# Kernel change: the last product's first weight unit is summed in DRAM and split early, with two output weightings in another order

## The chip, the cores and the metric

The kernel runs on one core of one Trainium2 chip. The metric is the device time of one execution in microseconds; the figure before is the median of three runs.

## The reference, cut to what matters

One layer: a token mixer with three gated branches, then a squared-ReLU MLP, each between RMS norms, over 512 tokens of 1024 channels in float32. The change lies in the MLP and the output.

```python
h = rms_norm(x, norm_ffn_pre[l])
f = jnp.square(jax.nn.relu(h @ w_ff1[l])) @ w_ff2[l]      # (512, 1024) @ (1024, 4096), then @ (4096, 1024)
x = x + rms_norm(f, norm_ffn_post[l])
```

## The kernel before, in words

**Numbers.** Each float32 operand is split in two parts: ScalarE copies it to a rounded "hi" part (`copy_hi`, L699), VectorE subtracts to get the "lo" part (`lo`, L1101), and TensorE makes three matmuls for each pair, hi by hi, hi by lo, lo by hi (L1621, L1623, L1625 in `products`; L1816, L1818, L1820 in `up_unit`).

**Weight units.** Weights come as units of 128 x 1024 values (512 KB). A unit is loaded from DRAM to one of ten slots in SBUF, split into one of four ring places of `w_hi` and `w_lo` (`RING = 4`), and used. The counts `w_hi_ready`, `w_lo_ready` and `unit_done` run over all units in order.

**The MLP.** The hidden width is worked in four quarters (`q`), each with a first matrix (`UP`, `w_ff1`) and a second one (`DOWN`, `w_ff2`). Each of these eight matrix products is made by a seven-product scheme of the Strassen kind over 2 x 2 blocks. `ORDER` gives the order: UP 1, 2, 5, 3, 6, 7, 4 and DOWN 5, 1, 2, 3, 6, 7, 4. A product needs a set of activations (a block, or a sum or difference of blocks, also split hi and lo, `set_hi`, `set_lo`) and a weight block or a sum of weight blocks in two units (h = 0, 1). The sums of weights come about in two ways: those of products 5 and 7 are made ahead in DRAM (`weight_sums`), during the mixer, by a plain copy issued on ScalarE's queue and a DMA with addition issued by GpSimd (`second_block`, L610); those of products 6 and 4 by adding one more block with such a DMA (`add_block`, L676) on top of the sum that already lies in the slot, once its split is done. The slots that DOWN 5, 6 and 4 use are 8 and 9 (`raw_d`), those of UP 5, 6 and 4 are 4 and 5 (in `glu`). So DOWN 4 of a quarter multiplies by the sum of all four blocks.

**Order of work.** Every engine's program is written out by hand. On ScalarE and VectorE, `split_behind(q, f, product, h)` splits the unit that comes four units later, once the unit named is done (for DOWN, once the product is done): behind UP 6 come the units of UP 4, behind UP 7 those of DOWN 5, behind UP 4 those of DOWN 1, behind DOWN 6 those of DOWN 4. SyncE's queue issues the loads in order (`ff_load`), each behind a wait for the split that frees its slot. A DOWN product is made in two tiles, t = 0 and 1, of 128 tokens by 512 columns each, 12 matmuls a tile; both need both units.

**The end.** In the last quarter each square (128 tokens `c` by half the columns) of the MLP's sum is finished by its last product: product 6 for c = 2 and 3, second half, product 7 for c = 0 and 1, second half, product 4 for c = 0 and 1, first half. Per tile VectorE adds the tile to the sum (`add_product`, L1463), ScalarE squares and sums it (`sum_squares`, L725) and, when a row block is whole, takes a root (L1093). VectorE multiplies each half by the norm's gain (`weigh`, L1468), takes the reciprocal of the root (L1477), scales, adds the residual and so releases the output DMA (`finish`, L1480, L561). `finish(n)` treats row block `FINAL[n]`, in the order 2, 3, 0, 1.

**Room.** `a_hi` and `a_lo` hold three differences of x blocks in the MLP; the second one, "21-22-11", is read by UP 6 alone.

Of the kernel before, what the change touches and what calls it, by code (L numbers as in the profile page):

```python
# [30 lines left out]
P = 128  # L31
# [63 lines left out]
MATRICES = 2 * QUARTERS  # L95
SLOTS = 10


# [131 lines left out]
def build(nc, x_d, xt_d, units_d, cols_d, rows_d, ws_d, bs_d, wsr_d, out_d):  # L230
    kept_d = nc.dram_tensor("mixed_kept", (SEQ, D), F32, kind="Internal").ap()
    made_d = nc.dram_tensor("weight_sums", (MATRICES * MADE_UNITS, P, D), F32, kind="Internal").ap()
    col_sums_d = nc.dram_tensor("spatial_sums", (KT, P), F32, kind="Internal").ap()
    with ExitStack() as ctx:
# [108 lines left out]
        last_weighted = {2: end[:, 1, :], 3: end[:, 2, :], 0: end[:, 3, :], 1: over("end_a", [P, D], "a_hi")}  # L343


        raw_loaded = [sem(f"raw_loaded{n}") for n in range(SLOTS)]
        first_copied = [sem(f"first_copied{f}") for f in range(2)]
        made = {product: sem(f"made{product}") for product in MADE}
        raw_added = [sem(f"raw_added{n}") for n in range(SLOTS)]
# [111 lines left out]
        def _(sp):  # L461
# [72 lines left out]
            for q in range(QUARTERS):  # L534
                if q == 1:
                    behind_sums(0, DOWN, 6)
                if q:
                    for product in (5, 1, 2, 3):
                        if product == 1:
                            ff_load(q, UP, 1, (0,))  # L540
                            behind_sums(q - 1, DOWN, 4)
                            ff_load(q, UP, 1, (1,))
                        else:
                            ff_load(q, UP, product)
                    ff_load(q, UP, 7)
                for product in (5, 1, 2, 3):
                    if q == 0 and product == 5:
                        behind_sums(0, UP, 6)
                    ff_load(q, DOWN, product)
                ff_load(q, DOWN, 7)  # L550
            sp.wait_ge(unit_done, ff_unit(QUARTERS - 1, UP, 4, 1) + 1)
# [14 lines left out]
        def _(pool):  # L566
# [37 lines left out]
            def second_block(m, product):  # L604
# [7 lines left out]
                               accum_op=ALU.add, max_dma_last_dim=SUM_BYTES).then_inc(made[product], 16)  # L612

            def mask_spatial(slot, loads):

                pool.wait_ge(spatial_loaded[slot], loads)
                nc.gpsimd.affine_select(out=ws_raw[:, slot, :], in_=ws_raw[:, slot, :],
                                        compare_op=ALU.is_ge, fill=0.0, base=0, pattern=[[1, P]],
                                        channel_multiplier=-1).then_inc(ws_masked, 1)
# [47 lines left out]
            for m in range(KT // 2, MATRICES):  # L667
                pool.wait_ge(unit_done, U_GATE + 2 * (KT + m) + 2)
                second_block(m, 7)

            def add_block(q, f, product, halves=(0, 1)):
# [11 lines left out]
            for q in range(QUARTERS):  # L683
                for f in range(2):
                    add_block(q, f, 6)
                    add_block(q, f, 4)

# [9 lines left out]
        def _(act):  # L697
# [11 lines left out]
            def ff_hi(u, into=None, free=True):  # L709
# [7 lines left out]
                if free:  # L717
                    act.wait_ge(unit_done, u + 1 - RING)
                copy_hi(w_hi[:, u % RING, :] if into is None else into, slots[slot]).then_inc(w_hi_ready, 1)

# [255 lines left out]
            def split_behind(q, f, product, h):  # L976
                u = ff_unit(q, f, product, h) + RING
                if u < UNITS:
                    ff_hi(u)
# [23 lines left out]
            for q in range(QUARTERS):  # L1003
# [46 lines left out]
                for h in range(2):  # L1050
                    done(q, UP, 7, h)
                    split_behind(q, UP, 7, h)
                act.wait_ge(hidden_diff, 4 * q + 1)
                set_hi(q, "22-21")
# [43 lines left out]
        def _(dve):  # L1098
# [12 lines left out]
            def ff_lo(u, into=None, hi=None):  # L1111

                dve.wait_ge(w_hi_ready, u + 1)
                lo(w_lo[:, u % RING, :] if into is None else into, slots[ff_slot(u)],
                   w_hi[:, u % RING, :] if hi is None else hi).then_inc(w_lo_ready, 1)

# [308 lines left out]
            def split_behind(q, f, product, h):  # L1425
                u = ff_unit(q, f, product, h) + RING
                if u < UNITS:
                    ff_lo(u)
# [57 lines left out]
            for q in range(QUARTERS):  # L1486
# [65 lines left out]
                split_behind(q, UP, 7, 1)  # L1552
                set_lo(q, "22-21")
                set_lo(q, "11")
                done(q, UP, 4, 0)
# [15 lines left out]
                for n, product in enumerate(ORDER[DOWN]):  # L1571
# [12 lines left out]
                    if q == QUARTERS - 1 and product == 4:  # L1584
                        dve.wait_ge(mlp_sum, sums_after(q, product, 0))
                        weigh(0, 0)
                        weigh(0, 1)
                        dve.wait_ge(out_weighted, 6)
# [17 lines left out]
                    elif product == 7:  # L1606
                        finish(1)
                    elif product == 4:
                        weigh(1, 1)
                        dve.wait_ge(mlp_sum, sums_after(q, product, 1))  # L1610
# [7 lines left out]
        def _(pe):  # L1618
# [207 lines left out]
            def down_tile(q, product, t):  # L1826
# [4 lines left out]
                for k in range(CH):  # L1831
                    u = ff_unit(q, DOWN, product, k // 2)
                    w = slice(k % 2 * HALF, (k % 2 + 1) * HALF)
                    mm = products(down_bank(q, product) + t, hi[:, k, at], low[:, k, at],
                                  w_hi[:, u % RING, w], w_lo[:, u % RING, w], k == 0 and not again,
                                  k == CH - 1, again)
# [24 lines left out]
            for q in range(QUARTERS):  # L1861
# [7 lines left out]
                for product in ORDER[DOWN]:  # L1869
                    for h in range(2):  # L1870
                        ready(Count(ff_unit(q, DOWN, product, h)))
                    pe.wait_ge(set_lo_ready, len(H_ORDER) * q + H_ORDER.index(SET_OF[product]) + 1)
# [63 lines left out]
```

## Time and profile before

| | |
|---|---|
| median of 3 runs | 953.14 us (953.08 to 953.18) |
| the profiled execution, its own time | 953.15 us |
| its span in the profile | 951.4 us (1.75 us of the time lie around it) |
| TensorE busy | 942.5 us, 99% |
| VectorE, ScalarE, GpSimd busy | 718.6, 431.8, 102.9 us |
| granted TensorE clock, mean | 0.999 of full speed (2.4 GHz) |

Times in the views are microseconds from the start of the span. In a timeline a line shows the start, the busy time, the engine, the source line, what is written and read and how many instructions are merged; in square brackets is the idle time before it and what ended that. The busy time of a VectorE or ScalarE instruction is a little longer than the distance to the next start when instructions follow each other without a pause, so distances between starts are used for chains.

### The profile page before, as it was taken

To read this page: it belongs to the slowest core of one execution; us is meant where nothing else is said; L and a number is where in the kernel's file an instruction comes from. 1 tells how busy PE (TensorE), PEld (TensorE's weight loads), DVE (VectorE), ACT (ScalarE), POOL (GpSimd) and SP (SyncE) were. 2 spreads that over 40 slices of the span, in tenths; PEclk is the share of its full clock that TensorE was granted. 3 is DMA by queue.
4 is the path that set the end of the run, shared out by engine and by line. 5 is a ranking of instruction groups with operands and counts; after the bars stand their busy time and mean duration, and the time that the engine had idled before them with its cause. 6 is when DMAs were issued, how large, how long until landed. Compare 5 with 4: busy or idle time off the path is not lost.

```text
span 951.4 us, 13451 instructions
## 1 busy us (share of the span) xinstructions
PE 942.5 (99%) x4824; PEld 807.5 (85%) x4824; DVE 718.6 (76%) x844; ACT 431.8 (45%) x536; POOL 102.9 (11%) x135
## 2 busy tenths in 40 slices
PE   9999999999999999999999999999999999999997
PEld 7888888888888888888888888899889989989985
DVE  5579879888888988886584444599975875786698
ACT  6543333333333322224374323377745745754774
POOL 1211001001100012222200000120001001100100
PEclk9999999999999999999999999999999999999999
DMA  8447558656755724454477323538586756848664
GB/s 319 141 160 229 172 169 229 186 189 193 196 187 176 199 89 132 132 134 153 134 194 248 111 89 112 198 129 236 167 253 133 235 171 154 229 133 244 187 191 132
DMA packets 41228, 168.01 MB, mean 177 GB/s; under 512 B 4953, under 2 KB 5089, under 8 KB 38881
## 3 DMA queue, kind: packets, MB, share of 16 engines
q1 hardware_dynamic: 31872, 111.85, 32.5%
q0 software_dynamic: 7680, 35.13, 20.8%
q10 hardware_dynamic: 1632, 20.45, 5.8%
q8 instruction: 27, 0.44, 0.2%
q14 instruction: 17, 0.13, 0.1%
HBM read 163.22 MB, written 37.75 MB: 211 GB/s over the span
## 4 chain that ended last, share of the span: by engine, by line
PE 97%; DVE 1%; DMA 1%; issue 0%; ACT 0%; SPq 0%; DVEq 0%
PE ps L1621 26%; PE ps L1625 26%; PE ps L1623 26%; PE ps L1816 6%; PE ps L1818 6%; PE ps L1820 6%; PE ps L1751 1%; DMA glu<-xt_in 1%; PE ps L1666 0%; DVE w_lo L1101 0%; DVE wide L1480 0%; DVE end L1468 0%; DVE wide L1463 0%; ACT c_hi L737 0%; DVE end_a L1468 0%
## 5 line engine op out<-in xcount | busy, mean ns | idle before, releaser
L1101 DVE TENSOR_TENSOR w_lo<-raw,w_hi 128x1024 fp32r<-128x1024 f32 (+1 forms) x141 | 172.3, 1227 | 93.8 <-ACT w_hi L699 93.5
L699 ACT ACTIVATE w_hi<-raw 128x1024 fp32r<-128x1024 f32 (+1 forms) x140 | 146.1, 1052 | 202.2 <-PE ps L1625 118.3
L1621 PE MATMUL ps<-a_hi,w_hi 128*128 128x512 f32 x576 | 224.9, 390 | 0.0
L1625 PE MATMUL ps<-a_hi,w_lo 128*128 128x512 f32 x576 | 224.2, 389 | 0.0
L1623 PE MATMUL ps<-a_lo,w_hi 128*128 128x512 f32 x576 | 224.1, 389 | 0.0
L1189 DVE SCALAR_TENSOR_TENSOR conf<-glu,cols,conf (+1 forms) x240 | 186.8, 778 | 27.5 <-DVE conf L1189 26.4
L1625 PEld LDWEIGHTS ps<-a_hi,w_lo 128*128 128x128 f32 x576 | 108.1, 188 | 22.6
L1623 PEld LDWEIGHTS ps<-a_lo,w_hi 128*128 128x128 f32 x576 | 108.2, 188 | 22.2
L1621 PEld LDWEIGHTS ps<-a_hi,w_hi 128*128 128x128 f32 x576 | 108.2, 188 | 22.2
L1621 PE MATMUL ps<-w_hi,h_hi 128*128 128x512 f32 x224 | 87.2, 389 | 0.0
L1623 PE MATMUL ps<-w_lo,h_hi 128*128 128x512 f32 x224 | 87.2, 389 | 0.0
L1625 PE MATMUL ps<-w_hi,h_lo 128*128 128x512 f32 x224 | 87.1, 389 | 0.0
L1816 PE MATMUL ps<-x_plain_hi,w_hi 128*128 128x256 f32 x256 | 72.6, 283 | 0.0
L1818 PE MATMUL ps<-x_plain_lo,w_hi 128*128 128x256 f32 x256 | 72.4, 283 | 0.0
L1820 PE MATMUL ps<-x_plain_hi,w_lo 128*128 128x256 f32 x256 | 72.4, 283 | 0.0
L1101 DVE TENSOR_TENSOR w_lo<-glu,w_hi 128x1024 fp32r<-128x1024 f32 x40 | 48.5, 1223 | 28.0 <-ACT w_hi L699 28.0
L699 ACT ACTIVATE w_hi<-glu 128x1024 fp32r<-128x1024 f32 x40 | 41.7, 1053 | 29.6 <-PE ps L1820 18.2
L1816 PE MATMUL ps<-x_diff_hi,w_hi 128*128 128x256 f32 x192 | 54.5, 284 | 0.0
L1818 PE MATMUL ps<-x_diff_lo,w_hi 128*128 128x256 f32 x192 | 54.3, 283 | 0.0
L1820 PE MATMUL ps<-x_diff_hi,w_lo 128*128 128x256 f32 x192 | 54.3, 283 | 0.0
L1621 PE MATMUL ps<-b_hi,w_hi 128*128 128x512 f32 x128 | 49.9, 390 | 0.0
L1625 PE MATMUL ps<-b_hi,w_lo 128*128 128x512 f32 x128 | 49.8, 389 | 0.0
(186 smaller groups left out, 1580.4 us busy)
## 6 DMA issues: line engine op xcount, KB each, us to landing
raw<-units_in SPq DMA_DIRECT2D x127, 512.0 KB, 3.3
weight_sums<-units_in POOLq DMA_DIRECT2D x16, 1024.0 KB, 7.8
raw_v<-units_in SPq DMA_DIRECT2D x16, 512.0 KB, 6.0
glu<-units_in SPq DMA_DIRECT2D x16, 512.0 KB, 7.5
raw<-weight_sums SPq DMA_DIRECT2D x16, 512.0 KB, 4.2
glu<-units_in POOLq DMA_DIRECT2D x16, 512.0 KB, 5.3
raw_d<-units_in POOLq DMA_DIRECT2D x16, 512.0 KB, 6.5
glu<-weight_sums SPq DMA_DIRECT2D x8, 512.0 KB, 5.5
```

What stands on the lines that cost most here:

```text
L699: return nc.scalar.activation(dst, src, ACT.Copy, scale=scale)
L1101: return nc.vector.tensor_tensor(dst, src, hi, ALU.subtract)
L1189: nc.vector.scalar_tensor_tensor(out=conf[:, tile, :], in0=glu[:, tile, k:k + SEQ], scalar=cols[:, tile, COL_CONF + k:COL_CONF + k + 1], i ...
L1621: nc.tensor.matmul(ps[:, bank, :], left_hi, right_hi, start=first, stop=False, skip_group_check=on_top)
L1623: nc.tensor.matmul(ps[:, bank, :], left_hi, right_lo, start=False, stop=False, skip_group_check=on_top)
L1625: return nc.tensor.matmul(ps[:, bank, :], left_lo, right_hi, start=False, stop=final, skip_group_check=on_top)
L1751: mm = nc.tensor.matmul(ps[:, 6, c * P:(c + 1) * P], v_tile[:, c, :], ws_raw[:, b, :], start=True, stop=True)
L1816: nc.tensor.matmul(out, w_hi[:, u % RING, w], hi[:, k, :], start=not free and k == 0, stop=False, skip_group_check=free)
L1818: nc.tensor.matmul(out, w_hi[:, u % RING, w], low[:, k, :], start=False, stop=False, skip_group_check=free)
L1820: mm = nc.tensor.matmul(out, w_lo[:, u % RING, w], hi[:, k, :], start=False, stop=k == CH - 1, skip_group_check=free)
```

## The change

It has four parts.

1. A fifth kind of weight sum: one more unit in `weight_sums` holds the sum for unit h = 0 of DOWN 4 in the last quarter (`EARLY`). GpSimd builds it by three DMAs, one behind each of the last `second_block` calls for products 7: a plain copy of block (1, 0), an addition of block (1, 1), and an addition of the sum already made for product 5.
2. SyncE loads it into slot 4, once UP 4's first unit of the last quarter has been split out of that slot, ahead of the loads of DOWN 2, 3 and 7. ScalarE splits it behind its split after UP 7, h = 0, and VectorE between the sets "22-21" and "11", into the second place of `a_hi` and `a_lo`.
3. At the end the split of that unit behind DOWN 6 is gone on both engines, as is the addition DMA for it. The counts are kept by an increment of 2 for the next unit. TensorE waits for `early_lo` and reads the unit from `a_hi`, `a_lo`.
4. Weightings: `weigh(0, 1)` moves from product 4's first tile to behind `finish(1)` in product 7, and `weigh(1, 1)` from behind product 4's second tile to its first.

```diff
+EARLY = UNITS - 2
+EARLY_SUM = MATRICES * MADE_UNITS
+EARLY_SLOT = 4
+EARLY_BLOCKS = ((1, 0), (1, 1))
...
+        early_w_hi, early_w_lo = resident(a_hi, 1), resident(a_lo, 1)
...
                     ff_load(q, DOWN, product)
+                    if q == QUARTERS - 1 and product == 1:
+                        sp.wait_ge(early_summed, 48)
+                        sp.wait_ge(w_lo_ready, ff_unit(q, UP, 4, 0) + 1)
+                        sp.dma_start(slots[EARLY_SLOT], made_d[EARLY_SUM]).then_inc(early_loaded, 16)
...
+            def early_step(n):
+
+                into = made_d[EARLY_SUM]
+                if n == 0:
+                    pool.dma_start(into, units_d[block_of(EARLY, EARLY_BLOCKS[0])]).then_inc(early_summed, 16)
+                elif n == 1:
+                    pool.wait_ge(early_summed, 16)
+                    pool.dma_start(into, units_d[block_of(EARLY, EARLY_BLOCKS[1])], accum_op=ALU.add,
+                                   max_dma_last_dim=SUM_BYTES).then_inc(early_summed, 16)
+                elif n == 2:
+                    pool.wait_ge(early_summed, 32)
+                    pool.wait_ge(made[5], 16 * MATRICES)
+                    pool.dma_start(into, made_d[(MATRICES - 1) * MADE_UNITS], accum_op=ALU.add,
+                                   max_dma_last_dim=SUM_BYTES).then_inc(early_summed, 16)
...
                 second_block(m, 7)
+                early_step(m - KT // 2)
...
-                    add_block(q, f, 4)
+                    add_block(q, f, 4, (1,) if (q, f) == (QUARTERS - 1, DOWN) else (0, 1))
...
+                        ).then_inc(w_hi_ready, 2 if u == EARLY + 1 else 1)
...
-                if u < UNITS:
+                if u < UNITS and u != EARLY:
                     ff_hi(u)
...
                     split_behind(q, UP, 7, h)
+                    if q == QUARTERS - 1 and h == 0:
+                        act.wait_ge(early_loaded, 16)
+                        copy_hi(early_w_hi, slots[EARLY_SLOT]).then_inc(early_hi, 1)
...
                 set_lo(q, "22-21")
+                if q == QUARTERS - 1:
+                    dve.wait_ge(early_hi, 1)
+                    lo(early_w_lo, slots[EARLY_SLOT], early_w_hi).then_inc(early_lo, 1)
                 set_lo(q, "11")
...
                         weigh(0, 0)
-                        weigh(0, 1)
+                        weigh(1, 1)
                         dve.wait_ge(out_weighted, 6)
                         finish(2, (0,))
...
                     elif product == 7:
                         finish(1)
+                        dve.wait_ge(mlp_sum, sums_after(q, product, 1))
+                        weigh(0, 1)
                     elif product == 4:
-                        weigh(1, 1)
                         dve.wait_ge(mlp_sum, sums_after(q, product, 1))
                         weigh(1, 0)
```

**The order at three places.** In these rows `wide` is the MLP's sum, `end` and `end_a` the weighted rows, `raw_d` the slots 8 and 9, `h` the hidden blocks. In the changed kernel the same calls stand a few lines lower: `lo` is L1137, `copy_hi` L731, `add_product` L1499, `weigh` L1504, the reciprocal L1513 and `finish` L1516.

VectorE before, from the sum of product 6's second tile to the end (first to last the rows of the trace from 933.50 us on):

```order
L1463 TENSOR_TENSOR wide<-wide,ps 128x512 [waits mlp_sum,unit_done]
L1468 TENSOR_TENSOR end<-wide,end 128x512 [waits mlp_sum]
L1101 TENSOR_TENSOR w_lo<-raw_d,w_hi 128x1024 [waits w_hi_ready]
L1468 TENSOR_TENSOR end<-wide,end 128x512 [waits mlp_sum]
L1101 TENSOR_TENSOR w_lo<-raw_d,w_hi 128x1024 [waits w_hi_ready]
L1463 TENSOR_TENSOR wide<-wide,ps 128x512 [waits mlp_sum,tile_done]
L1477 RECIPROCAL rstd<-rstd 128x1 [waits end_root,out_weighted]
L1480 SCALAR_TENSOR_TENSOR wide<-end,rstd,back 128x512 [waits end_rstd]
L1480 SCALAR_TENSOR_TENSOR wide<-end,rstd,back 128x512
L1463 TENSOR_TENSOR wide<-wide,ps 128x512 [waits mlp_sum,unit_done]
```

```order
L1463 TENSOR_TENSOR wide<-wide,ps 128x512 [waits mlp_sum,tile_done]
L1468 TENSOR_TENSOR end<-wide,end 128x512 [waits mlp_sum]
L1468 TENSOR_TENSOR end<-wide,end 128x512
L1477 RECIPROCAL rstd<-rstd 128x1 [waits end_root,out_weighted]
L1480 SCALAR_TENSOR_TENSOR wide<-end,rstd,back 128x512 [waits end_rstd]
L1463 TENSOR_TENSOR wide<-wide,ps 128x512 [waits mlp_sum,unit_done]
L1468 TENSOR_TENSOR end_a<-wide,end 128x512
L1468 TENSOR_TENSOR end_a<-wide,end 128x512 [waits mlp_sum]
L1480 SCALAR_TENSOR_TENSOR wide<-end,rstd,back 128x512
L1477 RECIPROCAL rstd<-rstd 128x1 [waits end_root,out_weighted]
L1480 SCALAR_TENSOR_TENSOR wide<-end_a,rstd,back 128x512 [waits end_rstd]
L1480 SCALAR_TENSOR_TENSOR wide<-end_a,rstd,back 128x512
```

VectorE with the change, the same stretch:

```order
L1499 TENSOR_TENSOR wide<-wide,ps 128x512 [waits mlp_sum,unit_done]
L1504 TENSOR_TENSOR end<-wide,end 128x512 [waits mlp_sum] x2
L1137 TENSOR_TENSOR w_lo<-raw_d,w_hi 128x1024 [waits w_hi_ready]
L1499 TENSOR_TENSOR wide<-wide,ps 128x512 [waits mlp_sum,tile_done]
L1513 RECIPROCAL rstd<-rstd 128x1 [waits end_root,out_weighted]
L1516 SCALAR_TENSOR_TENSOR wide<-end,rstd,back 128x512 [waits end_rstd]
L1516 SCALAR_TENSOR_TENSOR wide<-end,rstd,back 128x512
L1499 TENSOR_TENSOR wide<-wide,ps 128x512 [waits mlp_sum,unit_done]
```

```order
L1504 TENSOR_TENSOR end<-wide,end 128x512 [waits mlp_sum]
L1499 TENSOR_TENSOR wide<-wide,ps 128x512 [waits mlp_sum,tile_done]
L1504 TENSOR_TENSOR end<-wide,end 128x512 [waits mlp_sum]
L1504 TENSOR_TENSOR end_a<-wide,end 128x512
L1513 RECIPROCAL rstd<-rstd 128x1 [waits end_root,out_weighted]
L1516 SCALAR_TENSOR_TENSOR wide<-end,rstd,back 128x512 [waits end_rstd]
L1499 TENSOR_TENSOR wide<-wide,ps 128x512 [waits mlp_sum,unit_done]
L1504 TENSOR_TENSOR end_a<-wide,end 128x512 [waits mlp_sum]
L1516 SCALAR_TENSOR_TENSOR wide<-end,rstd,back 128x512
L1513 RECIPROCAL rstd<-rstd 128x1 [waits end_root,out_weighted]
L1516 SCALAR_TENSOR_TENSOR wide<-end_a,rstd,back 128x512 [waits end_rstd]
L1516 SCALAR_TENSOR_TENSOR wide<-end_a,rstd,back 128x512
```

One `w_lo<-raw_d` of two is gone ahead of the sum of product 7's first tile; a weighting stands before the sum of product 4's first tile, and between the sum of its second tile and the last reciprocal one weighting and one `finish` half are left instead of two and one.

ScalarE with the change, in UP 7 of the last quarter; before, the same rows stand there without the one that writes `a_hi`:

```order
L1028 ACTIVATE h_70<-h_70 128x1024 [waits joined]
L1030 ACTIVATE h_70<-h_70 128x1024 [waits rectified]
L731 ACTIVATE w_hi<-raw_d 128x1024 [waits unit_done,raw_loaded8]
L731 ACTIVATE a_hi<-glu 128x1024 [waits early_loaded]
L731 ACTIVATE w_hi<-raw_d 128x1024 [waits unit_done,raw_loaded9]
L731 ACTIVATE h_hi<-h_69 128x1024 [waits hidden_diff]
L1028 ACTIVATE h_71<-h_71 128x1024 [waits joined]
L1030 ACTIVATE h_71<-h_71 128x1024 [waits rectified]
```

The new copy waits for the early load and stands ahead of DOWN 5's second unit.

SyncE's queue with the change, in the last quarter; before, the same rows stand there without the one of L565:

```order
L529 DMA raw_d<-weight_sums 128x1024 [waits w_lo_ready] x2
L529 DMA raw<-units_in 128x1024 [waits w_lo_ready] x2
L565 DMA glu<-weight_sums 128x1024 [waits w_lo_ready,early_summed]
L529 DMA raw_v<-units_in 128x1024 [waits w_lo_ready] x2
L529 DMA glu<-units_in 128x1024 [waits w_lo_ready] x2
L529 DMA raw<-weight_sums 128x1024 [waits w_lo_ready] x2
L570 DMA end<-rows_in 128x1024 [waits mixed_kept2,mixed_kept1,mixed_kept3,mixed_kept0,unit_done]
```

The new load, with its wait, stands between the loads of DOWN 1 and of DOWN 2, 3 and 7.

## Rows read from the trace of the kernel before

**Rows 1.** Page part 4, shares of the chain that ended last
```profile
PE 97%; DVE 1%; DMA 1%; issue 0%; ACT 0%; SPq 0%; DVEq 0%
```

**Rows 2.** Waits of TensorE in the whole span: us in total, times, longest
```profile
PE ps L1691 <- POOL ones L570: 1.4, 1, 1.4
PE ps L1621 <- DVE w_lo L1101: 0.4, 1, 0.4
```

**Rows 3.** Timeline of TensorE, 925 to 952 us: last matmuls of two tiles
```profile
933.07 0.39 PE L1625 MATMUL ps<-w_hi,h_lo 128*128 128x512 f32 x1
...
943.95 0.39 PE L1625 MATMUL ps<-w_hi,h_lo 128*128 128x512 f32 x1
```

**Rows 4.** Timeline of VectorE, 900 to 952 us
```profile
933.50 0.69 DVE L1463 TENSOR_TENSOR wide<-wide,ps 128x512 f32<-128x512 f32 x1
...
934.83 1.22 DVE L1101 TENSOR_TENSOR w_lo<-raw_d,w_hi 128x1024 fp32r<-128x1024 f32 x1
...
936.57 1.22 DVE L1101 TENSOR_TENSOR w_lo<-raw_d,w_hi 128x1024 fp32r<-128x1024 f32 x1
937.70 0.68 DVE L1463 TENSOR_TENSOR wide<-wide,ps 128x512 f32<-128x512 f32 x1
938.30 0.16 DVE L1477 RECIPROCAL rstd<-rstd 128x1 f32<-128x1 f32 x1
...
939.82 0.68 DVE L1463 TENSOR_TENSOR wide<-wide,ps 128x512 f32<-128x512 f32 x1
...
941.95 0.68 DVE L1463 TENSOR_TENSOR wide<-wide,ps 128x512 f32<-128x512 f32 x1
942.66 1.29 DVE L1468 TENSOR_TENSOR end<-wide,end 128x512 f32<-128x512 f32 x2
943.99 0.16 DVE L1477 RECIPROCAL rstd<-rstd 128x1 f32<-128x1 f32 x1
...
944.86 0.68 DVE L1463 TENSOR_TENSOR wide<-wide,ps 128x512 f32<-128x512 f32 x1
945.45 1.29 DVE L1468 TENSOR_TENSOR end_a<-wide,end 128x512 f32<-128x512 f32 x2
946.66 0.74 DVE L1480 SCALAR_TENSOR_TENSOR wide<-end,rstd,back 128x512 f32<-128x512 f32 x1
947.32 0.15 DVE L1477 RECIPROCAL rstd<-rstd 128x1 f32<-128x1 f32 x1
947.51 1.41 DVE L1480 SCALAR_TENSOR_TENSOR wide<-end_a,rstd,back 128x512 f32<-128x512 f32 x2
```

**Rows 5.** Timeline of ScalarE, 900 to 952 us
```profile
900.60 1.06 ACT L699 ACTIVATE w_hi<-raw_d 128x1024 fp32r<-128x1024 f32 x1 [1.71 <-PE ps L1820]
...
933.58 2.02 ACT L699 ACTIVATE w_hi<-raw_d 128x1024 fp32r<-128x1024 f32 x2 [3.43 <-PE ps L1625]
...
937.52 0.29 ACT L1093 ACTIVATE rstd<-sumsq,meansq 128x1 f32<-128x1 f32 x1
...
946.32 0.29 ACT L1093 ACTIVATE rstd<-sumsq,meansq 128x1 f32<-128x1 f32 x1
```

**Rows 6.** Timeline of VectorE, 900 to 952 us, its earlier part
```profile
905.77 1.23 DVE L1101 TENSOR_TENSOR h_lo<-h,h_hi 128x1024 fp32r<-128x1024 f32 x1 [1.73 <-ACT h_hi L699]
...
913.92 2.35 DVE L1101 TENSOR_TENSOR w_lo<-raw_v,w_hi 128x1024 fp32r<-128x1024 f32 x2
```

**Rows 7.** Timeline of VectorE, 860 to 900 us
```profile
893.05 1.23 DVE L1101 TENSOR_TENSOR w_lo<-glu,w_hi 128x1024 fp32r<-128x1024 f32 x1 [0.15 <-ACT w_hi L699]
```

**Rows 8.** Page part 6, DMA issues of the whole span
```profile
raw<-units_in SPq DMA_DIRECT2D x127, 512.0 KB, 3.3
weight_sums<-units_in POOLq DMA_DIRECT2D x16, 1024.0 KB, 7.8
```

**Rows 9.** DMA issues, stretch 895 to 896.5 us: KB each, us to landing
```profile
glu<-units_in SPq DMA_DIRECT2D x1, 512.0 KB, 9.0
```

**Rows 10.** DMA issues, stretch 891 to 892.6 us
```profile
raw<-units_in SPq DMA_DIRECT2D x1, 512.0 KB, 5.4
```

More of the change, by code:

```diff
@@ L231, in build @@
     kept_d = nc.dram_tensor("mixed_kept", (SEQ, D), F32, kind="Internal").ap()
-    made_d = nc.dram_tensor("weight_sums", (MATRICES * MADE_UNITS, P, D), F32, kind="Internal").ap()
+    made_d = nc.dram_tensor("weight_sums", (MATRICES * MADE_UNITS + 1, P, D), F32, kind="Internal").ap()
     col_sums_d = nc.dram_tensor("spatial_sums", (KT, P), F32, kind="Internal").ap()
@@ L343, in build @@
         last_weighted = {2: end[:, 1, :], 3: end[:, 2, :], 0: end[:, 3, :], 1: over("end_a", [P, D], "a_hi")}
+        early_w_hi, early_w_lo = resident(a_hi, 1), resident(a_lo, 1)
         raw_loaded = [sem(f"raw_loaded{n}") for n in range(SLOTS)]
         first_copied = [sem(f"first_copied{f}") for f in range(2)]
+        early_summed = sem("early_summed")
+        early_loaded = sem("early_loaded")
+        early_hi = sem("early_hi")
+        early_lo = sem("early_lo")
         made = {product: sem(f"made{product}") for product in MADE}
@@ L718, in ff_hi @@
                     act.wait_ge(unit_done, u + 1 - RING)
-                copy_hi(w_hi[:, u % RING, :] if into is None else into, slots[slot]).then_inc(w_hi_ready, 1)
+                copy_hi(w_hi[:, u % RING, :] if into is None else into, slots[slot]
+                        ).then_inc(w_hi_ready, 2 if u == EARLY + 1 else 1)
             def after(u):
@@ L1114, in ff_lo @@
                 lo(w_lo[:, u % RING, :] if into is None else into, slots[ff_slot(u)],
-                   w_hi[:, u % RING, :] if hi is None else hi).then_inc(w_lo_ready, 1)
+                   w_hi[:, u % RING, :] if hi is None else hi).then_inc(w_lo_ready, 2 if u == EARLY + 1 else 1)
             def after(u):
@@ L1426, in split_behind @@
                 u = ff_unit(q, f, product, h) + RING
-                if u < UNITS:
+                if u < UNITS and u != EARLY:
                     ff_lo(u)
@@ L1833, in down_tile @@
                     w = slice(k % 2 * HALF, (k % 2 + 1) * HALF)
+                    unit_hi, unit_lo = ((early_w_hi, early_w_lo) if u == EARLY else
+                                        (w_hi[:, u % RING, :], w_lo[:, u % RING, :]))
                     mm = products(down_bank(q, product) + t, hi[:, k, at], low[:, k, at],
-                                  w_hi[:, u % RING, w], w_lo[:, u % RING, w], k == 0 and not again,
+                                  unit_hi[:, w], unit_lo[:, w], k == 0 and not again,
                                   k == CH - 1, again)
@@ L1870, in _ @@
                     for h in range(2):
-                        ready(Count(ff_unit(q, DOWN, product, h)))
+                        u = ff_unit(q, DOWN, product, h)
+                        if u == EARLY:
+                            pe.wait_ge(early_lo, 1)
+                        else:
+                            ready(Count(u))
                     pe.wait_ge(set_lo_ready, len(H_ORDER) * q + H_ORDER.index(SET_OF[product]) + 1)
```

## The prediction

> **What bounds the kernel now.** I read the chain of waits first: 97% of the chain that ended last is TensorE [rows 1]. Then TensorE's own waits: it waited twice in the whole span, 1.4 us for constants at the start and 0.4 us for one split [rows 2]. Its matmuls are not changed in number or kind, so outside the start there are 0.4 us to be won on TensorE, and everything else must come from the end. There I read TensorE's timeline. The last matmuls of two tiles, four tiles apart, start at 933.07 and 943.95 us [rows 3], so a tile takes (943.95 - 933.07) / 4 = 2.72 us and a product 5.44. VectorE takes up the first of these tiles at 933.50 [rows 4], 0.43 after that last matmul's start, without being late. By the same 0.43 the four tiles after it are ready at 936.22 and 938.94 (product 7), 941.66 and 944.38 (product 4). VectorE's timeline shows when it takes them up: 937.70, 939.82, 941.95 and 944.86 [rows 4], so 1.48, 0.88, 0.29 and 0.48 us late. After TensorE's last tile the end is VectorE's queue alone: sum, two weightings, half of a finish, reciprocal at 947.32, two halves of the last finish from 947.51, and the output's DMA until 951.4.
>
> **The change, part by part.**
>
> *The split that goes from the end.* The two splits of the last units start at 934.83 and 936.57, the sum of product 7's first tile at 937.70 [rows 4]: one split is worth 937.70 - 936.57 = 1.13. Without it that sum starts at 936.57 (ready since 936.22). The reciprocal behind it starts at 938.30 - 1.13 = 937.17 if ScalarE's root is there. The root was over at 937.52 + 0.29 = 937.81, but ScalarE loses one of two copies of together 2.02 us ahead of it [rows 5], so it is over near 936.8: no wait. The next sum was 939.82 - 937.70 = 2.12 later, which would be 938.69, but TensorE gives its tile at 938.94. So here the gain of 1.13 falls to 939.82 - 938.94 = 0.88, and VectorE is on time.
>
> *The weighting moved ahead of product 4's first sum.* That sum was 941.95 - 939.82 = 2.13 behind the one before it; now a weighting, 0.60 us (two take 946.66 - 945.45 = 1.21 [rows 4]), stands between as well: 938.94 + 2.13 + 0.60 = 941.67, ready at 941.66. Of the 0.88, 941.95 - 941.67 = 0.28 are left. The stretch to the last sum holds the same work as before (two weightings, a reciprocal, half a finish, 944.86 - 941.95 = 2.91): 944.58, ready at 944.38. The gain stays 0.28.
>
> *The weighting moved out from behind the last sum.* Before, the sum was followed after 0.59 by a weighting that needed nothing from it, then by the one that did. Now the dependent one stands directly behind. What that costs is seen at 941.95: the weighting that waits for that sum starts 0.71 later [rows 4]. So: 944.58 + 0.71 + 0.60 (weighting) + 0.66 (half a finish, 947.32 - 946.66) = 946.55 for the last reciprocal. Is the root there? Before, it was over at 946.32 + 0.29 = 946.61 [rows 5], 1.75 after the sum's start; now at 944.58 + 1.75 = 946.33, so VectorE still sets it, by 0.22. Gain: 947.32 - 946.55 = 0.77, of which 0.28 is the split and 0.49 the order (0.60 less 0.11 for the exposed wait).
> The Trainium skill speaks to that 0.11. Its page "VectorE: DVE Perf Modes", section "The DRAIN you can't avoid", says that chained VectorE operations pay a pipeline flush with or without semaphores and that a semaphore between them costs nothing extra. By that rule the gain would be 0.88. The trace disagrees (0.71 against 0.59 for the same instruction), and I keep the rows.
>
> *The split put into UP 7.* ScalarE's copy stands ahead of the split at 900.60, before which it sat idle for 1.71 us [rows 5]; a copy is half of 2.02, some 1.0. It fits if the unit has landed by about 899.6. VectorE's subtraction, 1.13, stands ahead of the set at 905.77, before which it sat idle for 1.73 [rows 6], so 0.6 of idle time is left. Cost: none, as long as ScalarE is in time. The cover behind it is thin: VectorE then works without a pause worth naming until the splits of DOWN 2, over at 913.92 + 2.35 = 916.27 [rows 6], which TensorE wants at 943.95 + 0.23 - 5 x 5.44 = 916.98 (0.23 is a twelfth of a tile). So 0.7 us of lateness is free, and what exceeds it stalls TensorE one for one.
>
> *The early load.* SyncE may issue it when the split that starts at 893.05 [rows 7] is over, near 894.3. What stands behind it in SyncE's queue, the loads of DOWN 2, 3 and 7, is delayed by 1.5 to 2 us; DOWN 2 is split by VectorE only from 913.92 on [rows 6], so that costs nothing. How long the early load takes is not in the trace. Nearest from below is the median load, 3.3 us [rows 8]; from above, a load issued at the end of this same burst, 9.0 us [rows 9]; nearest in place, one issued 2 us before it with others right behind, 5.4 us [rows 10]. I take 5.4: landing at 899.7, 0.1 after the free point and inside the 0.7. Cost 0; with 3.3 also 0; with 9.0 see the second rival.
>
> *The sum in DRAM.* Three DMAs of 512 KB are added behind three transfers of 1 MB that land in 7.8 us [rows 8] and are issued, by the waits on TensorE's units, two units of 5.44 us or 10.9 us apart. GpSimd's waits for the previous step are therefore over when it comes to them, and the last of the three is done long before it is loaded. Weight loads beside them could be slower, yet TensorE waited for no load while sixteen such 1 MB transfers ran [rows 2, 8]. Bounds: nothing to gain, and the 0.4 us of the one wait as a loss. I take 0.
>
> *The addition that goes* (one of two 512 KB DMAs ahead of the last splits) frees nothing: the copies there start when TensorE's product is done, not at a landing [rows 5].
>
> *Sum:* 953.15 - 0.28 - 0.49 = **952.4 us** (952.38) against the profiled execution's own 953.15, which is within 0.01 us of the median of 953.14. A difference of 0.2% (1.9 us) is about the least that a measurement of this kernel can tell from no change; this one is 0.08%.
>
> **The rivals.**
> 1. *The split's share is lost, the order's stays.* Anything that holds VectorE up to 0.3 us before product 4 (a root that comes late, work pushed back by the subtraction in UP 7) eats the 0.28: 953.15 - 0.49 = 952.7; with both shares lost, 953.15. For it: the margins are 0.2 to 0.3 us. Against it: after 938.94 VectorE is paced by TensorE again, which clears older debts. Chance 0.13.
> 2. *The early load comes late and ScalarE's queue stands behind it.* This is the one that ends on the slow side. With 9.0 us it lands at 903.3, 3.7 after 899.6. ScalarE's split of DOWN 5's second unit, the sets and VectorE's splits all wait behind it; less the 0.7 and what short idle times give, TensorE stalls 2.9 us before DOWN 2: 953.15 + 2.9 - 0.77 = 955.3. It decides from a landing later than 900.3 (6.0 us) on, and is slower than before from 7 us on. For it: the load of the same burst that took 9.0 [rows 9]. Against it: that one was the sixth of the burst (two units each of DOWN 1, 2 and 3), the early one is the third. Chance 0.06 for more than 0.2% slower, 0.02 for less.
> The Trainium skill's page "DMA: Bandwidth & Descriptors", section "Issuing engines are not separate DMA queues", says that DMAs from all issuing engines run on the same 16 engines and interleave; by it the early load shares them with whatever is under way, which the spread of 3.3 to 9.0 us bears out.
> 3. *The exposed wait costs nothing* (the rule of the flush above): weighting 0.60 after the sum, reciprocal at 946.44, time 952.3. Against it stand the rows at 941.95 and 944.86. Chance 0.04.
> 4. *The change gives more.* Even with VectorE never late, the last root needs 1.75 from the last tile: 944.38 + 1.75 = 946.13, a gain of 1.19, time 952.0; with the 0.4 of TensorE's one wait, 951.6. So faster by over 0.2% (below 951.2) has no mechanism: chance 0.01.
>
> **How the numbers follow.** The forecast has 0.74, the rivals 0.13, 0.08, 0.04 and 0.01. The range runs from 952.0, the limit without stalls, to 953.2, both shares lost: it leaves out the late load and little else. Faster by over 0.2%: 0.01. Within 0.2%: 0.93. Slower by over 0.2%: 0.06.
>
> **What would show it.** In the changed profile: TensorE waits still 1.8 us in all, none behind the early subtraction; one copy in ScalarE's former 1.71 of idle time and one subtraction in VectorE's 1.73; the early load landing within 6 us; from TensorE's last matmul as zero, the last sum at +0.63 (before +0.91), the last reciprocal at +2.60 (before +3.37) and the span's end at +6.7 (before +7.45). The prediction is wrong if the early copy ends an idle time that a DMA released and TensorE shows a stall between 906 and 917 us, if the last reciprocal waits for the root, or if the matmuls themselves change pace.

## The result, and the profile after

| | before | with the change |
|---|---|---|
| median of 9 runs | 953.18 us | 956.37 us |
| lowest and highest | 953.08, 953.57 | 954.13, 958.70 |
| profiled execution, its own time and span | 953.15, 951.4 us | 954.13, 952.4 us |

The ratio is 1.0032, with a 95% interval of 1.0024 to 1.0041: slower by 0.3%. The change is also unsteady, over 4.6 us where the kernel before varies by 0.5, and its profiled execution is the fastest of its nine. That profile can show the mechanism, then, but only at the smallest cost that it had in these runs.

The page's span and chain of the change:

```profile
span 952.4 us, 13457 instructions
...
PE 94%; DVE 2%; DMA 2%; ACT 2%; issue 1%; SPq 0%; DVEq 0%; ACTq 0%
```

Against [rows 1] TensorE's share fell from 97 to 94%, and DMA and ScalarE came into the chain. Who TensorE waited for (us in total, times, longest):

```profile
PE ps L1661 <- DVE b_lo L1138: 1.8, 1, 1.8
PE ps L1731 <- POOL ones L586: 1.4, 1, 1.4
PE ps L1661 <- DVE w_lo L1137: 0.9, 1, 0.9
PE ps L1741 <- ACT c_hi L770: 0.4, 1, 0.4
```

Against [rows 2] two of these are the kernel's first microseconds (w_lo, c_hi), where executions differ by some tenths and make it up before 100 us. The new one is 1.8 us for `b_lo`, the lo parts of the second branch, which stand at the end of ScalarE's and VectorE's layer norm work near 505 us. From 100 to 475 us both traces run alike, to 0.01 us. With the change ScalarE is then held once by a late load (its split at 485.63 instead of 485.03), which its idle time before the next splits makes up; the second time it isn't. ScalarE before (start, busy, and the idle time in front with its releaser), and with the change:

```profile
495.91 1.06 ACT L699 ACTIVATE w_hi<-raw 128x1024 fp32r<-128x1024 f32 x1 [2.71 <-PE ps L1625]
...
502.36 2.18 ACT L699 ACTIVATE b_hi<-glu 128x512 fp32r<-128x512 f32 x4
```

```profile
497.77 1.07 ACT L731 ACTIVATE w_hi<-raw 128x1024 fp32r<-128x1024 f32 x1 [3.97 <-DMA raw<-units_in]
...
504.22 2.18 ACT L731 ACTIVATE b_hi<-glu 128x512 fp32r<-128x512 f32 x4
```

The same weight split starts 1.86 us later, no longer released by TensorE but by the landing of a load, and the copies to `b_hi` that end the layer norm follow 1.86 later. So do VectorE's `b_lo`, before and with the change:

```profile
503.10 2.49 DVE L1102 SCALAR_TENSOR_TENSOR b_lo<-glu,b_hi 128x512 fp32r<-128x512 f32 x4
```

```profile
504.96 2.49 DVE L1138 SCALAR_TENSOR_TENSOR b_lo<-glu,b_hi 128x512 fp32r<-128x512 f32 x4
```

The load, issued in the stretch 487.5 to 489.5 us (KB, us to landing), before and with the change:

```profile
raw<-units_in SPq DMA_DIRECT2D x1, 512.0 KB, 7.1
```

```profile
raw<-units_in SPq DMA_DIRECT2D x1, 512.0 KB, 9.4
```

Beside it, issued 485 to 490 us, are the transfer of 1 MB that was there before and the third of the new DMAs:

```profile
weight_sums<-units_in POOLq DMA_DIRECT2D x1, 1024.0 KB, 9.0
weight_sums<-weight_sums POOLq DMA_DIRECT2D x1, 512.0 KB, 11.8
```

So the load took 9.4 instead of 7.1 us beside them. There was no slack behind it: before, TensorE's weight load (PEld) had already waited for the same `b_lo`, in the stretch 495 to 510 us:

```profile
PEld ps L1621 <- DVE b_lo L1102: 0.3, 1, 0.3
```

The end went a little better than forecast, counted from TensorE's last matmul. That matmul and VectorE's timeline with the change:

```profile
945.82 0.39 PE L1665 MATMUL ps<-w_hi,h_lo 128*128 128x512 f32 x1
```

```profile
938.43 0.68 DVE L1499 TENSOR_TENSOR wide<-wide,ps 128x512 f32<-128x512 f32 x1
939.03 0.15 DVE L1513 RECIPROCAL rstd<-rstd 128x1 f32<-128x1 f32 x1
...
940.80 0.69 DVE L1499 TENSOR_TENSOR wide<-wide,ps 128x512 f32<-128x512 f32 x1 [0.17 <-PE ps L1665]
...
943.53 0.68 DVE L1499 TENSOR_TENSOR wide<-wide,ps 128x512 f32<-128x512 f32 x1
944.25 0.69 DVE L1504 TENSOR_TENSOR end<-wide,end 128x512 f32<-128x512 f32 x1
944.86 0.68 DVE L1504 TENSOR_TENSOR end_a<-wide,end 128x512 f32<-128x512 f32 x1
945.46 0.15 DVE L1513 RECIPROCAL rstd<-rstd 128x1 f32<-128x1 f32 x1
...
946.32 0.68 DVE L1499 TENSOR_TENSOR wide<-wide,ps 128x512 f32<-128x512 f32 x1
947.03 0.69 DVE L1504 TENSOR_TENSOR end_a<-wide,end 128x512 f32<-128x512 f32 x1
947.64 0.74 DVE L1516 SCALAR_TENSOR_TENSOR wide<-end,rstd,back 128x512 f32<-128x512 f32 x1
948.30 0.15 DVE L1513 RECIPROCAL rstd<-rstd 128x1 f32<-128x1 f32 x1
```

Counted from the last matmul's start, the last sum came at 946.32 - 945.82 = 0.50 (forecast 0.63, before 0.91 by [rows 3, 4]), the last reciprocal at 948.30 - 945.82 = 2.48 (forecast 2.60, before 3.37), the span's end at 952.4 - 945.82 = 6.6 (forecast 6.7, before 7.45). In UP 7 things stand about as counted; the early load took the 5.4 us that were taken for it. ScalarE's and VectorE's timelines:

```profile
901.55 1.06 ACT L731 ACTIVATE a_hi<-glu 128x1024 fp32r<-128x1024 f32 x1 [0.86 <-DMA glu<-weight_sums]
902.51 1.05 ACT L731 ACTIVATE w_hi<-raw_d 128x1024 fp32r<-128x1024 f32 x1
```

```profile
905.87 1.22 DVE L1137 TENSOR_TENSOR a_lo<-glu,a_hi 128x1024 fp32r<-128x1024 f32 x1
907.67 1.23 DVE L1137 TENSOR_TENSOR h_lo<-h,h_hi 128x1024 fp32r<-128x1024 f32 x1 [0.59 <-ACT h_hi L731]
```

This whole stretch is 1.8 us later than before, so the copy at 901.55 answers to 899.7. A load released it, one of the prediction's two signs of being wrong, but 0.1 after the free point, and the other sign, a stall of TensorE behind it, isn't there. VectorE kept 0.59 of its 1.73 us of idle time [rows 6].

### The profile page after: what moved, and what is told of

Same layout as the page of the kernel before. It is cut to its first block, busy times and chain, and to the rows that moved or that the text cites. A ratio compares the mean times of both kernels' runs of the same rounds, so it can differ in the third digit from the quotient of the medians.

```text
span 952.4 us, 13457 instructions
## 1 busy us (share of the span) xinstructions
PE 941.7 (99%) x4824; PEld 806.9 (85%) x4824; DVE 719.3 (76%) x844; ACT 431.9 (45%) x536; POOL 103.9 (11%) x137
## 4 chain that ended last, share of the span: by engine, by line
PE 94%; DVE 2%; DMA 2%; ACT 2%; issue 1%; SPq 0%; DVEq 0%; ACTq 0%
PE ps L1661 25%; PE ps L1663 25%; PE ps L1665 25%; PE ps L1856 6%; PE ps L1858 6%; PE ps L1860 6%; DMA raw<-units_in 1%; PE ps L1791 1%; DMA glu<-xt_in 1%; ACT w_hi L731 1%; DVE w_lo L1137 0%; ACT glu L924 0%; PE ps L1706 0%; DVE y_s L1362 0%; ACT conf L928 0%
## 5 line engine op out<-in xcount | busy, mean ns | idle before, releaser
L1137 DVE TENSOR_TENSOR w_lo<-raw,w_hi 128x1024 fp32r<-128x1024 f32 (+1 forms) x141 | 172.5, 1228 | 93.7 <-ACT w_hi L731 93.4
L731 ACT ACTIVATE w_hi<-raw 128x1024 fp32r<-128x1024 f32 (+1 forms) x140 | 146.0, 1052 | 204.2 <-PE ps L1665 115.6
L1137 DVE TENSOR_TENSOR w_lo<-glu,w_hi 128x1024 fp32r<-128x1024 f32 x40 | 48.5, 1222 | 28.1 <-ACT w_hi L731 28.1
L731 ACT ACTIVATE w_hi<-glu 128x1024 fp32r<-128x1024 f32 x40 | 41.8, 1054 | 29.7 <-PE ps L1860 18.2
L1663 PE MATMUL ps<-b_lo,w_hi 128*128 128x512 f32 x128 | 49.8, 389 | 0.0
```

The lines of the kernel that those rows point to most:

```text
L731: return nc.scalar.activation(dst, src, ACT.Copy, scale=scale)
L1137: return nc.vector.tensor_tensor(dst, src, hi, ALU.subtract)
L1663: nc.tensor.matmul(ps[:, bank, :], left_hi, right_lo, start=False, stop=False, skip_group_check=on_top)
```

## The experiments

Two theories stood against each other. A: the three DMAs that make the sum in DRAM delay weight loads while the second gates are made, and ScalarE's queue, the b parts and TensorE wait behind one of them. B: the early load and its copies in UP 7 cost it, in the executions that were not profiled. Each kernel ran beside the kernel before on the same chip (medians there 953.19, 953.19 and 953.25 us in the three groups of runs, e1 to e4, e5 to e8, e9 and e10).

**e1: the DMAs alone**, on the kernel before.

```diff
+            sp.wait_ge(early_summed, 48)
             for c in range(CH):
                 sp.wait_ge(mixed_kept[c], 16)
...
                 second_block(m, 7)
+                early_step(m - KT // 2)
```

> The kernel before, with nothing added but the three DMAs that make the early sum in DRAM (nobody uses it). Theory A (these DMAs delay a weight load that ScalarE's queue waits for while the gates are made, so the b parts come late and TensorE waits for them): slower than before by about the whole 3.2 us of the change plus its gain of 0.77, 955.5 to 958 us, unsteady from run to run, with a wait of TensorE for b_lo of 1.5 us or more near 505 us. Theory B (the early load and copies in UP 7 cost it in the runs that were not profiled): 953.2 us, steady, no such wait.

Measured: 955.84 us (954.57 to 957.75), ratio 1.0030 (1.0019 to 1.0041). TensorE's waits, and the load near 488 us:

```profile
PE ps L1715 <- POOL ones L578: 1.4, 1, 1.4
PE ps L1645 <- DVE b_lo L1126: 1.3, 1, 1.3
PE ps L1645 <- DVE w_lo L1125: 0.9, 1, 0.9
```

```profile
raw<-units_in SPq DMA_DIRECT2D x1, 512.0 KB, 8.9
```

Nobody uses these DMAs' result, yet they bring 2.65 of the change's 3.19 us of slowdown, with a spread of 3.2 us. Theory A stands. The wait in the profile, 1.3 us, is under the 1.5 expected; again the profiled execution was the fastest.

**e2: all but the DMAs.** The early unit then lacks two of its blocks; its load, its copies and the rest are those of the change.

```diff
-                        sp.wait_ge(early_summed, 48)
...
-                        sp.dma_start(slots[EARLY_SLOT], made_d[EARLY_SUM]).then_inc(early_loaded, 16)
+                        sp.dma_start(slots[EARLY_SLOT], made_d[(MATRICES - 1) * MADE_UNITS]).then_inc(early_loaded, 16)
...
-                early_step(m - KT // 2)
```

> The changed kernel without the three DMAs; the early unit is loaded from the sum already made for product 5, so the blocks (1, 0) and (1, 1) are left out of this weight unit. Everything in UP 7 and at the end is as in the change. Theory A: the forecast comes true, 952.4 us (952.2 to 952.7), steady, TensorE's wait for b_lo gone. Theory B: about 956 us and unsteady, as the change.

Measured: 952.72 us (952.09 to 953.35), ratio 0.9994 (0.9985 to 1.0003), no wait for `b_lo`. Theory B falls as an account of the 3 us. But the median misses the forecast by 0.3, just outside the range expected, and the eleven runs are scattered over 1.3 us, where 27 of the 29 runs of the kernel before beside them lie within 0.55 us (952.93 to 953.48, the other two at 954.2). So something small is left.

**e3: the order of the weightings alone.**

```diff
                         weigh(0, 0)
-                        weigh(0, 1)
+                        weigh(1, 1)
...
                         finish(1)
+                        dve.wait_ge(mlp_sum, sums_after(q, product, 1))
+                        weigh(0, 1)
                     elif product == 4:
-                        weigh(1, 1)
```

> The kernel before with the two weightings moved as in the change and nothing else. By the sum of the prediction the order is worth 0.49 us and the split 0.28: but here the weighting ahead of product 4's first sum adds 0.60 to a VectorE that was 0.29 late there, so the last sum comes at 944.86 + 0.60 = 945.46 and the last reciprocal at 945.46 + 0.71 + 0.60 + 0.66 = 947.43, 0.11 later than before: 953.25 us. A rival: the order alone is worth 0.49, 952.7 us.

Measured: 953.23 us (952.96 to 953.43), ratio 1.0000. As reckoned from the rows, alone it is worth nothing.

**e4: the DMAs later**, behind units of the third gates.

```diff
                 second_block(m, 7)
-                early_step(m - KT // 2)
+
+            for n in range(3):
+                pool.wait_ge(unit_done, U_GATE + 4 * KT + 4 * (n + 1))
+                early_step(n)
```

> The changed kernel with the three DMAs issued after the gates of the third branch have begun, one every 21.8 us behind no other transfer with addition. Theory A, if it is the coincidence with the 1 MB transfers and ScalarE's layer norm work that costs: 952.4 us, steady, and faster than both kernels. If any such DMA beside the weight loads costs: 953 us or more. Theory B: about 956 us.

Measured: 952.78 us (952.29 to 953.80), ratio 0.9996 (0.9987 to 1.0005). No wait for `b_lo` either, but the "952.4 us, steady" that was expected is missed by 0.4. The same three DMAs cost 3.6 us in one place (956.37 less 952.78) and none of that in the other. The spread of e2 is here as well, and UP 7 shows where from. ScalarE's timeline:

```profile
900.01 1.06 ACT L734 ACTIVATE a_hi<-glu 128x1024 fp32r<-128x1024 f32 x1 [1.14 <-DMA glu<-weight_sums]
900.98 1.04 ACT L734 ACTIVATE w_hi<-raw_d 128x1024 fp32r<-128x1024 f32 x1
```

The early load, 5.7 us on its way, released the copy at 900.01, after the free point of 899.6; everything behind it on ScalarE and VectorE came 0.4 later, and TensorE lost 0.24 us at DOWN 3's first matmuls (its last matmul starts at 944.19 instead of 943.95). In e2 the copy came at 900.29 and the last matmul at 944.48. This is the second rival of the prediction at a small size.

**e5: ScalarE's order in the second gates**, the DMAs where the change has them.

```diff
-                behind_branch(u)
+                if j < 6:
+                    behind_branch(u)
...
                     nc.scalar.activation(conf[:, t, :], nrm[:, t, :], ACT.Tanh,
                                          scale=0.5).then_inc(silu_th, 1)
+                if j >= 6:
+                    behind_branch(u)
```

> The changed kernel, its three DMAs where the change has them; only on ScalarE, for j = 6 and 7 of the second gates, the layer norm's scaling and tanh stand ahead of the weight split that waits for a late load, instead of behind it. Theory A with its path (late load, ScalarE's queue head, b parts, TensorE): the wait for b_lo near 505 us goes although the loads are as late as before, 952.7 us, about as the kernel with the late DMAs. If the DMAs cost in another way as well: above 954 us.

Measured: 958.23 us (957.87 to 959.51), ratio 1.0056 (1.0043 to 1.0070). The expectation was wrong. TensorE's wait, and VectorE's timeline:

```profile
PE ps L1664 <- DVE b_lo L1141: 3.8, 1, 3.8
```

```profile
503.42 1.23 DVE L1140 TENSOR_TENSOR w_lo<-raw,w_hi 128x1024 fp32r<-128x1024 f32 x1 [3.48 <-ACT w_hi L731]
504.56 2.49 DVE L1380 SCALAR_TENSOR_TENSOR glu<-conf,glu 128x512 f32<-128x512 f32 x4
506.96 2.49 DVE L1141 SCALAR_TENSOR_TENSOR b_lo<-glu,b_hi 128x512 fp32r<-128x512 f32 x4
```

I had looked at ScalarE's queue only. VectorE multiplies `glu` behind the lo part of the weight split, so the split that I moved back on ScalarE (to 502.34) now held VectorE until 503.42, and the b parts came later than ever, without ScalarE waiting for any DMA. The load near 488 us moved as well (issued near 491, 6.8 us). The run says nothing against theory A, and bears out one link of it: TensorE waits when the b parts are late, whatever makes them so. That a better order would hide the late load was not tried further.

**e6: only the third DMA later.**

```diff
-                early_step(m - KT // 2)
+                if m - KT // 2 < 2:
+                    early_step(m - KT // 2)
+            pool.wait_ge(unit_done, U_GATE + 4 * KT + 4)
+            early_step(2)
```

> The changed kernel with only the third DMA (addition of the sum from DRAM to DRAM) issued later; the copy and the first addition stay. If the third alone costs, since it runs beside the load issued near 488 us: 952.8 us. If each of them costs: between 952.8 and 956, with a wait for b_lo of under 1 us or none in the profile but some slower executions.

Measured: 952.83 us (952.34 to 953.40), ratio 0.9997 (0.9988 to 1.0006), as e4. The load near 488 us:

```profile
raw<-units_in SPq DMA_DIRECT2D x1, 512.0 KB, 6.5
```

It is the third DMA that costs. The second lengthens a load as well (the one issued near 478 us took 6.1 us, in e4 3.7, before 4.2) and holds ScalarE's split back to 485.81 (before 485.03), but ScalarE's next split that counts, at 495.99, is released by TensorE again, and TensorE doesn't wait.

**e7: the DMAs late, and the early load alone on SyncE's queue.**

```diff
                         sp.dma_start(slots[EARLY_SLOT], made_d[EARLY_SUM]).then_inc(early_loaded, 16)
+                        sp.wait_ge(early_loaded, 16)
```

> The changed kernel with the three DMAs late (as in e4) and with SyncE waiting for the early load to land before it issues the loads of DOWN 2 and 3. In e4's profile the early load took 5.7 us beside them, ScalarE copied at 900.01 and TensorE lost some 0.24 us at DOWN 3. Alone it should land in 3.3 to 4.5 us, by 898.8, ScalarE's copy comes at 898.8 and the loss goes: 952.4 us median and less spread than e4's 952.3 to 953.8. If the residual spread has another cause: 952.8 us again.

Measured: **952.32 us** (952.10 to 952.46), ratio 0.9991 (0.9982 to 1.0000). All 11 runs lie under the lowest of the 27 runs of before (953.07). The early load, and ScalarE's timeline:

```profile
glu<-weight_sums SPq DMA_DIRECT2D x1, 512.0 KB, 3.9
```

```profile
898.84 1.04 ACT L735 ACTIVATE a_hi<-glu 128x1024 fp32r<-128x1024 f32 x1
900.64 1.06 ACT L735 ACTIVATE w_hi<-raw_d 128x1024 fp32r<-128x1024 f32 x1 [0.76 <-PE ps L1864]
```

The copy follows the split in front of it without waiting, the next one is released by TensorE again, the spread is gone, and the last matmul starts at 944.00. VectorE's last reciprocal:

```profile
946.49 0.15 DVE L1517 RECIPROCAL rstd<-rstd 128x1 f32<-128x1 f32 x1
```

This is the time that was forecast for the change, met to 0.1 us, and the version that beats both kernels.

**e8: copies in place of the additions**, otherwise as e1.

```diff
-                    pool.dma_start(into, units_d[block_of(EARLY, EARLY_BLOCKS[1])], accum_op=ALU.add,
-                                   max_dma_last_dim=SUM_BYTES).then_inc(early_summed, 16)
+                    pool.dma_start(into, units_d[block_of(EARLY, EARLY_BLOCKS[1])]).then_inc(early_summed, 16)
...
-                    pool.dma_start(into, made_d[(MATRICES - 1) * MADE_UNITS], accum_op=ALU.add,
-                                   max_dma_last_dim=SUM_BYTES).then_inc(early_summed, 16)
+                    pool.dma_start(into, made_d[(MATRICES - 1) * MADE_UNITS]).then_inc(early_summed, 16)
```

> As e1 (the kernel before with the three DMAs added, nobody uses the result), but the two additions are plain copies of the same 512 KB: the arithmetic of the early sum is left out. If the bytes and packets are what delays the weight loads: as e1, 955 to 956 us. If it is the addition: 953.2 to 954 us.

Measured: 953.75 us (953.36 to 954.33), ratio 1.0006 (0.9997 to 1.0015). The load near 488 us:

```profile
raw<-units_in SPq DMA_DIRECT2D x1, 512.0 KB, 8.0
```

```profile
PE ps L1643 <- DVE b_lo L1124: 0.4, 1, 0.4
```

Copies cost 0.6 us where additions cost 2.7 (e1), and the load takes 8.0 us instead of 8.9. So the bytes alone bring a part, and most comes with the addition. A copy also drops the packet size that the additions ask for; whether the adding or the packets cost is not told apart by this.

The profiles so far fit one line: with the load at 8.0, 8.9 and 9.4 us (e8, e1, the change) TensorE waits 0.4, 1.3 and 1.8 us for `b_lo`, each time the excess over some 7.6 us, the 7.1 of before and the 0.5 us of slack behind it.

**e9: e7 with the old order of weightings.**

```diff
                         weigh(0, 0)
-                        weigh(1, 1)
+                        weigh(0, 1)
...
                         finish(1)
-                        dve.wait_ge(mlp_sum, sums_after(q, product, 1))
-                        weigh(0, 1)
                     elif product == 4:
+                        weigh(1, 1)
```

> The kernel of e7 with the weightings in the order of before, so that the removed split acts alone. By the prediction's sum the last sum still comes 0.28 us earlier, and from it to the last reciprocal it takes the 2.46 us of before instead of 1.97: 0.5 us slower than e7, 952.8 to 952.9 us, a gain of 0.3 on before. If the order is worth nothing even with the split gone (as it was alone, in e3): 952.3 us.

Measured: 952.87 us (952.80 to 954.15), ratio 0.9997 (0.9988 to 1.0006): 0.55 above e7. The profiles give the shares free of the spread between executions. From the last matmul's start to the last reciprocal it takes 3.37 us before, 947.04 - 943.95 = 3.09 here, and 946.49 - 944.00 = 2.49 in e7: the split alone is worth 0.28, the order 0.60 on top of it and nothing without it (e3). The medians agree to 0.1 (0.38 against the 953.25 beside it, and 0.55). VectorE's timeline shows one more part of the order's share:

```profile
942.38 1.29 DVE L1508 TENSOR_TENSOR end<-wide,end 128x512 f32<-128x512 f32 x2
943.71 0.16 DVE L1517 RECIPROCAL rstd<-rstd 128x1 f32<-128x1 f32 x1
...
947.04 0.16 DVE L1517 RECIPROCAL rstd<-rstd 128x1 f32<-128x1 f32 x1
```

With the old order the reciprocal starts 1.33 us after the pair of weightings, with the new one 945.46 - 944.25 = 1.21. The reciprocal waits for the sixth weighting; in the old order that is the one right in front of it, in the new one it is one earlier.

**e10: the early load behind those of DOWN 2 and 3**, otherwise as e4.

```diff
-                    if q == QUARTERS - 1 and product == 1:
+                    if q == QUARTERS - 1 and product == 3:
                         sp.wait_ge(early_summed, 48)
```

> The kernel of e4 (the three DMAs late) with the early load issued behind those of DOWN 2 and 3 instead of ahead of them. It prices the second rival: landing near 904 us, ScalarE's copy some 4.2 us after the free point of 899.6, TensorE stalled by 4.2 less 0.7, about 3.3 to 3.6 us, ahead of DOWN 2: 955.6 to 956.2 us. If the queues behind ScalarE's wait have more slack than I counted: below 955.

Measured: 956.34 us (955.62 to 957.08), ratio 1.0033 (1.0022 to 1.0045). ScalarE's copy, and TensorE's longest wait:

```profile
904.24 1.06 ACT L734 ACTIVATE a_hi<-glu 128x1024 fp32r<-128x1024 f32 x1 [5.30 <-DMA glu<-weight_sums]
```

```profile
PE ps L1664 <- DVE h_lo L1140: 2.6, 1, 2.6
```

The load landed 8.7 us after its issue, and the copy came 904.24 - 899.6 = 4.6 after the free point. TensorE's last matmul starts at 948.38 in this profile, 4.4 later than before; the median, 0.1 above the range expected, is 3.6 above e4's. So lateness stalls TensorE one for one, as the second rival had it, but only some 0.2 us of it is free, not 0.7. e4 and e2 say the same at small sizes: 0.41 late loses 0.24, 0.69 late loses 0.53, and here 4.64 late loses 4.43.

## Why the prediction was wrong

**The sum in DRAM** is the step that failed: "Bounds: nothing to gain, and the 0.4 us of the one wait as a loss. I take 0." It cost 2.7 us alone (e1, 955.84 against 953.19) and 3.6 in the change (956.37 less the 952.78 of e4); the 0.9 between the two is less than the spread of either kernel, and no run explains it. Its evidence was that TensorE waited for no load while sixteen transfers of 1 MB ran. But that TensorE never waited does not show that a load had slack. A load has three queues in front of TensorE, and the trace before held the sign in each: ScalarE's split at 495.91 was released by TensorE with the load landed only 0.5 us earlier (issued near 488.3, 7.1 us), its layer norm work stood behind that split, and TensorE's weight load had just begun to wait for the last b part. I asked whether GpSimd would be held and whether the sum would be ready, and both answers were right. I did not ask which load is in flight beside each of the three DMAs and who stands behind it, though for the load in UP 7 I did just that.

**The upper end of the range** followed from it: 953.2 held both shares lost and no cost of the DMAs. The bound was the largest wait seen, not the cost of the nearest case, a weight load made 2 or 3 us later by a DMA beside it. The 0.06 given to "slower by over 0.2%" stood for the early load alone; the result went there by another path. Of the signs named ahead only one pointed to it: TensorE's waits were to be still 1.8 us in all, and are 1.8 + 1.4 + 0.9 + 0.4 = 4.5.

**The split and the order** were right in mechanism and nearly in size (forecast 0.77, from the profiles 3.37 - 2.48 = 0.89; e7 against before 953.19 - 952.32 = 0.87). The split's 0.28 is borne out by e9 (0.28 by the profiles). The order was given 0.49 and brought 0.60 by the profiles, 0.55 by the medians; the missing term is the 0.12 of the wait on the sixth weighting. [rows 4] had it: the reciprocal 943.99 - 942.66 = 1.33 behind a pair of weightings, and an operation that waits for no weighting 946.66 - 945.45 = 1.21. The exposed wait behind the last sum was 947.03 - 946.32 = 0.71 us, as the rows said. The Trainium skill's page "VectorE: DVE Perf Modes", section "The DRAIN you can't avoid", by which a semaphore between chained operations costs nothing, does not hold here for an operation that waits for the one directly in front: it starts 0.71 after it, against 0.59 to 0.61 for those that don't wait. So the third rival, built on that rule, did not come true.

**The first rival** (the split's share lost) did not come true once the DMAs were away. **The second** was right in mechanism (e10), and in a small form is what e2, e4 and e6 are short of: landings at 5.9 and 5.7 us lost 0.53 and 0.24. Its price was too low, since the forecast had called 0.7 us of lateness free and 0.2 is (e10). For DOWN 2 the 0.7 was worked out rightly, but DOWN 3 binds first, and that was not reckoned. VectorE's splits for DOWN 3 in the kernel before:

```profile
919.72 2.36 DVE L1101 TENSOR_TENSOR w_lo<-glu,w_hi 128x1024 fp32r<-128x1024 f32 x2
```

They are over at 922.08, and TensorE is due to start DOWN 3 at 943.95 + 0.23 - 4 x 5.44 = 922.42: by the prediction's own reckoning 0.34 us, not 0.7 (the runs show 0.2). In e4 they are over at 920.08 + 2.35 = 922.43. e7 removes the lateness.

**The fourth** (more gain) did not happen, and its limit of 1.19 stands.

What stays open: the executions of the change that took 955.5 to 958.7 us have no profile. That their longer times are the same wait for `b_lo`, only longer, is likely, since moving the third DMA away removes both the median's loss and most of that spread (e6), but it was not seen. Nor was it tried whether the addition would cost as much without the 1 MB transfer 0.5 us ahead of it.

## What to carry to other kernels

A background DMA is not free because the bottleneck engine never waited for a load. Find each load in flight beside it, the instruction that takes it up, and what is queued behind that instruction, and compare the load's landing with the moment at which it is needed; and follow the path over all engines, since moving one engine's wait can hold another's (e5). Put such transfers where the loads have slack, and give an urgent load the queue to itself: here one wait of the issuing queue turned 5.7 us into 3.9 and took 0.46 us (952.78 to 952.32) and the spread of 1.5 us away.

## What the runs showed of the hardware

- The same 512 KB addition from DRAM to DRAM, issued 0.5 us behind one of 1 MB, made a plain load on another queue 9.4 us long (8.9 in e1, 8.0 beside plain copies in e8, 7.1 before, and 6.5 to 7.2 in the profiles with the third DMA absent or later).
- With the three DMAs in that place the time varied from one execution to the next by several microseconds (954.13 to 958.70; 954.57 to 957.75 in e1, which adds nothing else). With them later and the early load alone on its queue all 11 executions lie within 0.4 (e7).
- A load of 512 KB, directly ahead of four others on the same queue, landed after 5.4 to 5.9 us (the change, e2, e4, e6); with the four held back until it had landed, after 3.9 and 4.6 (e7, e9). So here loads issued later on the same queue delayed an earlier one.
